# Four whole-expert weight buffers on SyncE's queue and the down weights on ScalarE's, in a mixture-of-experts layer

## The reference

```python
h = layer_norm(ALPHA * h + rglru_mixer(h), ...)
idx, w = route(h)                       # top 8 of 64 experts for each token
for block, e in blocks_of_rows_by_expert:          # routed experts
    gu = x[rows] @ w_gu[e]              # 1024 -> 2 x 256
    y = ((silu(gu[:, :256]) * gu[:, 256:]) @ w_down[e]) * row_weight
    acc = acc.at[rows].add(y)
ffn = acc + swiglu(x, sh_w_gu, sh_w_down)          # the shared expert
h = layer_norm(ALPHA * h + ffn, ...)
```

## Time and profile before

| | us |
|---|---|
| median of three runs | 1255.48 |
| the three runs | 1253.23 to 1258.09 |
| profiled execution, its own time | 1257.67 |
| its span | 1255.8 |
| mean granted TensorE clock, of full speed | 0.983 |
| TensorE matmul busy | 1190.0 |
| VectorE busy | 787.9 |
| GpSimd busy | 604.0 |
| ScalarE busy | 421.6 |
| gate/up weight loads (128 of 1 MB) | 8.4 median to landing |
| down weight loads (64 of 1 MB) | 9.0 median to landing |

### The profile page before, as it was taken

How to read it: one execution, slowest core, us unless ns; L and a number is a source line. 1 busy time by engine, 2 the same in 40 slices (tenths; PEclk the granted TensorE clock), 3 DMA queues, 4 the chain that set the end, 5 groups by cost and what they waited for, 6 DMA issues and landing times.

```text
span 1255.8 us, 22625 instructions
## 1 busy us (share of the span) xinstructions
PE 1190.0 (95%) x7122; PEld 1040.9 (83%) x7122; DVE 787.9 (63%) x1625; ACT 421.6 (34%) x582; POOL 604.0 (48%) x509
## 2 busy tenths in 40 slices
PE   6999999999999699999999999999999999999983
PEld 6897989747874289999999999999999998988941
DVE  7565647288987155666666666565666656647638
ACT  5253434353441023233233233232232232323323
POOL 5222222001657356556556656565666656646310
PEclk9999999999999999999999999999999999999987
DMA  6111111403341799999999999999999999999854
GB/s 240 51 35 51 49 35 34 188 22 135 104 166 40 277 321 335 380 363 358 376 360 353 374 355 353 357 355 360 348 355 353 343 353 347 345 341 315 273 132 177
DMA packets 83587, 317.50 MB, mean 253 GB/s; under 512 B 15989, under 2 KB 32450, under 8 KB 58594
## 3 DMA queue, kind: packets, MB, share of 16 engines
q1 hardware_dynamic: 56592, 249.50, 51.3%
q0 software_dynamic: 26656, 67.23, 21.9%
q10 hardware_dynamic: 306, 0.34, 0.1%
HBM read 274.38 MB, written 51.00 MB: 259 GB/s over the span
## 4 chain that ended last, share of the span: by engine, by line
DMA 49%; PE 24%; issue 11%; DVE 7%; POOL 3%; ACT 2%; POOLq 1%; DVEq 0%; ACTq 0%; SPq 0%
DMA routed_rows<-ysb,to_row 46%; PE bank L116 6%; PE bank L117 6%; PE bank L118 6%; PE bank L440 2%; PE bank L954 2%; POOL expert_list L784 1%; DMA xg<-h_rows,from_row 1%; PE bank L895 1%; POOL xg L809 1%; DMA win_raw<-in_w_in 1%; POOL routed_rows L839 1%; DVE routed L1437 1%; DVE routed L1426 1%; DVE h L1133 1%
## 5 line engine op out<-in xcount | busy, mean ns | idle before, releaser
L954 PEld LDWEIGHTS bank<-xT,wgu 128*128 128x128 f32 x4096 | 515.7, 191 | 24.3 <-issue 12.6
L954 PE MATMUL bank<-xT,wgu 128*128 128x160 f32 (+1 forms) x4096 | 520.2, 288 | 13.9 <-DVE sh L1230 11.8
L809 POOL DMA_INDIRECT xg<-h_rows,from_row x288 | 323.3, 1123 | 113.4 <-issue 86.4
L839 POOL DMA_INDIRECT routed_rows<-ysb,to_row x96 | 147.4, 1535 | 216.0 <-issue 211.3
L1095 ACT ACTIVATE ysb<-bank,of_row 128x512 f32<-128x512 f32 x64 | 44.0, 687 | 403.0 <-DVE to_row L1309 334.5
L1356 DVE TENSOR_TENSOR wd_lo<-wd_raw,wd_hi 128x1024 fp32r<-128x1024 f32 x128 | 151.2, 1222 | 35.9 <-ACT wd_hi L1086 35.4
L1086 ACT ACTIVATE wd_hi<-wd_raw 128x1024 fp32r<-128x1024 f32 x128 | 127.9, 1048 | 1.4 <-issue 0.6
L784 POOL DMA_INDIRECT expert_list<-entry,place x64 | 64.6, 1010 | 129.6 <-DVE place L1194 111.9
L116 PE MATMUL bank<-hT_hi,win_hi 128*128 128x348 f32 (+1 forms) x320 | 113.5, 355 | 9.6 <-DVE hT_lo L538 9.6
L116 PE MATMUL bank<-wd_hi,hid_hi 128*128 128x512 f32 x256 | 107.8, 421 | 7.3 <-DVE wd_lo L1356 7.2
L352 POOL TENSOR_TENSOR win_lo<-win_raw,win_hi 128x1024 fp32r<-128x1024 f32 x16 | 43.4, 2715 | 145.9 <-ACT win_hi L463 145.9
(11 more groups left out here) (216 smaller groups left out, 1640.3 us busy)
## 6 DMA issues: line engine op xcount, KB each, us to landing
wgu<-in_w_gu SPq DMA_DIRECT2D x128, 1024.0 KB, 8.4
wd_raw<-in_w_down SPq DMA_DIRECT2D x64, 1024.0 KB, 9.0
win_raw<-in_w_in SPq DMA_DIRECT2D x16, 512.0 KB, 3.9
xg<-h_rows,from_row POOLq DMA_INDIRECT x288
hT_raw<-in_hT SPq DMA_DIRECT2D x8, 520.0 KB, 7.8
wout_raw<-in_w_out SPq DMA_DIRECT2D x1, 4096.0 KB, 13.9
h_in<-in_h_rows SPq DMA_DIRECT2D x8, 512.0 KB, 4.0
h_rows<-h SPq DMA_DIRECT2D x8, 512.0 KB, 2.7
```

The costliest lines, as they stand in the source:

```text
L809: pool.indirect_dma_start(out=xg[b][:, g, :], out_offset=None, in_=h1_quarters, in_offset=bass.IndirectOffsetOnAxis(ap=from_row[b][:, g:g ...
L839: pool.indirect_dma_start(out=routed_rows, out_offset=bass.IndirectOffsetOnAxis(ap=to_row[b][0:r, half:half + 1], axis=0), in_=ysb[b][0:r, ...
L954: mm = pe.matmul(bank[:, 2 * f + half, 0:BLOCK[b]], wgu[b][:, f, k, c:c + P], xT[b][:, k, 0:BLOCK[b]], start=(k == 0), stop=(k == KT - 1))
```

## The change

Gate/up weights get four buffers of a whole expert. Two of them lie where `h1` and the mixer's tiles were, which is why SyncE waits for `h1_stored`, `routed_begun` and `turned` before it fills the third. One DMA of 2 MB loads an expert, on one semaphore, and that of block t+4 is asked for when up(t) is done. SyncE's step holds nothing else. The down weights of block t+2 are asked for by ScalarE, on its own DMA queue, as the last thing of its step t and after `down_done` of t; the first two are still SyncE's. At the start SyncE sends only the gate/up weights of block 0, waits for `lists_loaded`, then sends the down weights of 0 and the gate/up weights of 1 and 2; the gate/up weights of 3 go behind the rest of the lists. ScalarE's `gate(1)` goes ahead of its wait for `sched_stored`, VectorE's `gate_shared(1)` ahead of its first transpose. The loop's body is four steps instead of two, and the number of blocks is rounded up to a multiple of four; an empty block is added where that is needed (four more small VectorE instructions).

```diff
-T_MAX = 2 * (HALF + SEQ * TOP_K // P)
+BUFS = 4
+T_MAX = 2 * (HALF + SEQ * TOP_K // P) + 2
...
-    wgu = [m.at(f"wgu{j}", 16384 * j, [P, FT, KT, 2 * P], F32) for j in range(2)]
+    wgu_at = (0, 16384, 166432, 182816)
+    wgu = [m.at(f"wgu{j}", wgu_at[j], [P, FT, KT, 2 * P], F32) for j in range(BUFS)]
...
+    def wgu_loads(i, j):
+        return i * 16 // BUFS + j // BUFS * 16 + 16
...
+    def load_wd(eng, i, j):
+        e = of_block(eng, i + j, 1, E - 1)
+        eng.dma_start(wd_raw[j % 2][:, :, :],
+                      w_down[bass.ds(e, 1)].rearrange("o p k c -> p (o k) c")
+                      ).then_inc(wd_loaded[j % 2], 16)
...
-        n = eng.value_load(sched_i[0:1, 5:6], min_val=E - 4, max_val=T_MAX - 4)
-        with eng.Fori(0, n, 2) as i:
-            for b in range(2):
-                yield i, b, 4
-        for j in range(4):
-            yield n, j, 3 - j
+        n = eng.value_load(sched_i[0:1, 5:6], min_val=E - BUFS, max_val=T_MAX - BUFS)
+        with eng.Fori(0, n, BUFS) as i:
+            for j in range(BUFS):
+                yield i, j, 4
+        for j in range(BUFS):
+            yield n, j, BUFS - 1 - j
...
-        load_wgu(0, 0, 0)
-        load_wgu(0, 0, 1)
-        load_wd(0, 0)
-        load_wgu(0, 1, 0)
-        load_wgu(0, 1, 1)
+        load_wgu(0, 0)
+
+        sp.wait_ge(lists_loaded, 16 * NQ)
+        load_wd(sp, 0, 0)
+        load_wgu(0, 1)
+
+        sp.wait_ge(h1_stored, 16 * TILES)
+        sp.wait_ge(routed_begun, 16 * TILES)
+        sp.wait_ge(turned, TILES)
+        load_wgu(0, 2)
         sp.wait_ge(sh_up, 2 * FT)
-        load_wd(0, 1)
+        load_wd(sp, 0, 1)
...
+        load_wgu(0, 3)
...
-        for f in range(FT):
-            sp.wait_ge(up_done, UPS + 2 * f + 2)
-            load_wgu(0, 2, f)
         sp.wait_ge(sched_loaded, 16)
         for i, j, more in steps(sp):
-            for f in range(FT if more >= 3 else 0):
-                sp.wait_ge(up_done, (i + j) * UPS + 2 * UPS + 2 * f + 2)
+            if more >= 4:
+                sp.wait_ge(up_done, (i + j) * UPS + 2 * UPS)
                 sp.sem_inc(sp_pass, 1)
-                load_wgu(i, j + 3, f)
-            if more >= 2:
-                sp.wait_ge(down_done, DOWNS[1] + before(DOWNS, i, j + 1))
-                sp.sem_inc(sp_pass, 1)
-                load_wd(i, j + 2)
+                load_wgu(i, j + 4)
...
         act.dma_start(sched_dram[HALF:, :], sched_i[HALF:, 0:4]).then_inc(sched_stored, 16)
+        gate(1)
         act.wait_ge(sched_stored, 16)
...
-        gate(1)
...
+            if more >= 2:
+
+                act.wait_ge(down_done, DOWNS[1] + before(DOWNS, i, j + 1))
+                act.sem_inc(act_pass, 1)
+                load_wd(act, i, j + 2)
...
         rows_from(0, 1)
+        gate_shared(1)
         turn(0, 0)
         rows_from(0, 2)
-        gate_shared(1)
```

More of the change, by code:

```diff
@@ L73 @@
 HALF = E // 2
-T_MAX = 2 * (HALF + SEQ * TOP_K // P)
-assert T_MAX <= 2 * P
+BUFS = 4
+T_MAX = 2 * (HALF + SEQ * TOP_K // P) + 2
+assert T_MAX <= 2 * P and E % BUFS == 0
 UPS = 2 * FT
@@ L645, in stores_to @@
         return loads(i, j) * STORES[j % 2] + 16 * (j % 2)
+    def wgu_loads(i, j):
+        return i * 16 // BUFS + j // BUFS * 16 + 16
     def loads(i, j):
         return i * 8 + j // 2 * 16 + 16
-    wgu_loaded = [[sem(f"wgu_loaded{j}_{f}") for f in range(FT)] for j in range(2)]
+    wgu_loaded = [sem(f"wgu_loaded{j}") for j in range(BUFS)]
     wd_loaded = [sem(f"wd_loaded{j}") for j in range(2)]
@@ L679, in build @@
     sp_pass, pool_pass, pe_pass = sem("sp_pass"), sem("pool_pass"), sem("pe_pass")
-    dve_pass = sem("dve_pass")
+    dve_pass, act_pass = sem("dve_pass"), sem("act_pass")
+    def load_wd(eng, i, j):
[3 more added lines that the diff above has]
+                      ).then_inc(wd_loaded[j % 2], 16)
     def blocks_to_run(eng):
@@ L730, in experts_sp, with load_wgu @@
         sp.wait_ge(first_ready, 1)
-        def load_wgu(i, j, f):
+        def load_wgu(i, j):
             e = of_block(sp, i + j, 1, E - 1)
[L734 to L742, removed]
-        load_wgu(0, 0, 0)
-        load_wgu(0, 0, 1)
-        load_wd(0, 0)
-        load_wgu(0, 1, 0)
-        load_wgu(0, 1, 1)
+            sp.dma_start(wgu[j % BUFS][:, :, :, :].rearrange("p f k c -> p (f k c)"),
+                         w_gu[bass.ds(e, 1)].rearrange("o p f k c -> p (o f k c)")
+                         ).then_inc(wgu_loaded[j % BUFS], 16)
+        load_wgu(0, 0)
[6 more added lines that the diff above has]
+        load_wgu(0, 2)
         sp.wait_ge(sh_up, 2 * FT)
-        load_wd(0, 1)
+        load_wd(sp, 0, 1)
         sp.dma_start(sdn[:, :, :], sh_down.rearrange("(k p) c -> p k c", p=P)
                      ).then_inc(sdn_loaded, 16)
-        sp.wait_ge(listed, 16 * TILES * TOP_K)
         for q in range(NQ):
@@ L945, in up @@
             pe.sem_inc(pe_pass, 1)
+            pe.wait_ge(wgu_loaded[j % BUFS], wgu_loads(i, j))
+            pe.sem_inc(pe_pass, 1)
             for f in range(FT):
-                pe.wait_ge(wgu_loaded[b][f], loads(i, j))
-                pe.sem_inc(pe_pass, 1)
                 pe.wait_ge(hid_ready, (i + j) * FT + f + 1)
@@ L954, in up @@
                         mm = pe.matmul(bank[:, 2 * f + half, 0:BLOCK[b]],
-                                       wgu[b][:, f, k, c:c + P], xT[b][:, k, 0:BLOCK[b]],
+                                       wgu[j % BUFS][:, f, k, c:c + P], xT[b][:, k, 0:BLOCK[b]],
                                        start=(k == 0), stop=(k == KT - 1))
@@ L1262, in experts_dve @@
         gate_shared(0)
-        s.step(dve.tensor_scalar(sched_i[:, 4:5], ends[:, E - 1:E], 2.0, float(E), ALU.mult,
-                                 ALU.add))
-        s.step(dve.tensor_scalar(sched_i[:, 5:6], sched_i[:, 4:5], 4, None, ALU.subtract))
+        s.step(dve.tensor_scalar(sched_i[:, 4:5], ends[:, E - 1:E], 1.0, None, ALU.add))
+        s.step(dve.tensor_scalar(sched_i[:, 4:5], sched_i[:, 4:5], 1, 2, ALU.logical_shift_right,
+                                 ALU.logical_shift_left))
+        s.step(dve.tensor_scalar(sched_i[:, 5:6], sched_i[:, 4:5], E - BUFS, None, ALU.add))
+        s.step(dve.tensor_scalar(sched_i[:, 4:5], sched_i[:, 4:5], E, None, ALU.add))
         s.step(dve.tensor_scalar(done, ends, extra, None, ALU.is_le))
@@ L1278, in experts_dve @@
         s.step(dve.tensor_reduce(sc(3), part, AX, ALU.add))
-        s.step(dve.scalar_tensor_tensor(sc(2), sc(6), float(COLS), sc(3), ALU.mult, ALU.add))
+        s.step(dve.tensor_scalar(sc(7), sc(4), E - 0.5, float(E), ALU.is_gt, ALU.mult))
+        s.step(dve.tensor_tensor(sc(7), sc(7), sc(3), ALU.add))
+        s.step(dve.scalar_tensor_tensor(sc(2), sc(6), float(COLS), sc(7), ALU.mult, ALU.add))
         s.step(dve.memset(sc(0), float(E)))
```

## The result

The changed kernel takes 1277.22 us (median of 4 runs, 1272.97 to 1280.36) against 1255.18 us before on the same chip: a ratio of 1.0187, 95% interval 1.0165 to 1.0209. It is slower by 22 us in the medians, where 1249.5 was forecast. Its profiled execution took 1272.97 us, with a span of 1271.0 us (before: 1257.67 and 1255.8). That is the fastest of its four runs, while the profiled run of the kernel before lies above its median, so the two traces differ by 15.2 us only.

The account below looks back on a forecast made before the run. Bound by TensorE and the chain of stores, within a few per cent. Start -4.5, ScalarE +1, loop 0, tail -2.5 sum to -6 us: from 1255.48 to 1249.5 us, range 1239 to 1268.

Parts of the forecast that it names:

- What bounds the kernel: Steady loop: TensorE at 23.30 us a pair and the chain of stores, within a few per cent; 9.3 us lost.
- the loop's sum of 0 + 1 us: Steady loop: 0 us for buffers and larger loads, +1 us for ScalarE asking for the down weights.
- Part 1: Gate/up loads: four whole-expert buffers, one 2 MB load; removes a wait of zero, taken as 0 us.
- Part 2: Down weights asked for by ScalarE: each step 0.7 us later, mostly hidden; loads land in 7 to 8 us; +1 us.
- What hides it is VectorE's wait for the store: ScalarE's 0.7 us a step is covered by VectorE's 3.80 us wait before even `picks`; uncovered, 43 us.
- Rival A: Loop: stores pay for the second weight queue and 16 KB runs, 12 to 25 us on top, 1262 to 1275; chance 0.20.
- My objection in the rival: Against slower stores in the loop: total bytes are fixed, and turns weights take early they don't need later; no size.
- my row-by-row account of it in the rival: With both weight queues busy, a store's row waits 0.32 + 0.64 us instead of 0.32; nine rows give +5.8 us.
- Part 3: Start: fewer weights sent before the lists, so lists land sooner and block 2 begins earlier; -4.5 us, bounds -9 and +5.
- Rival C: Start gives nothing: gathers stand behind 5 MB, or the rest of the lists holds VectorE; 1254 to 1260; chance 0.14.
- Tail: Last pairs: the last gate/up load goes out earlier, so stores at 1150 to 1185 us run with less beside them; -2.5 us.
- Rival D: Four-step loop body fetches its code again: 15 rounds at some 2 us, +30 us, 1280; chance 0.04.

Follow-up runs that it names:

- e1: Changed kernel with the loop's down weights asked for by SyncE again, on its own queue: 1291.39 us, ratio 1.0301 to before.
- e11: Changed kernel with gate/up weights of block t+3 asked for after up(t+1), the old time; ScalarE's queue and 16 KB runs stay: 1279.72 us, ratio 1.0200.
- e10: Changed kernel with down weights back on SyncE's queue and whole gate/up loads (16 KB runs) asked for at the old times: 1255.83 us, ratio 1.0014.
- e5: Changed kernel with down weights back on SyncE's queue and gate/up loads split into 8 KB runs, early requests kept: 1273.18 us, ratio 1.0139.
- e8: Changed kernel with down weights back on SyncE's queue, 8 KB runs, and gate/up halves asked for at the old times: 1253.49 us, ratio 0.9994.
- e2: Changed kernel with each 2 MB gate/up load split into two of 1 MB with 8 KB runs: 1264.51 us, ratio 1.0084.
- e13: Changed kernel with gate/up weights asked for at the old times and ScalarE asking for down weights before its wait for ysb: 1276.10 us, ratio 1.0143.
- e3: Kernel before with only the loop's down weights asked for by ScalarE, on its own queue at the end of its step: 1284.81 us, ratio 1.0148.
- e4: Kernel before with only the change's new order of the start: 1254.13 us, ratio 1.0002.
- e7: Kernel before with all weight loads cut to 4 KB runs: 1263.22 us, ratio 1.0072.
- e6: Changed kernel with ScalarE asking for down weights before its wait for ysb: 1281.65 us, ratio 1.0221.

## Why the prediction was wrong, step by step

**What bounds the kernel: right, but without its time.** Two bounds within a few per cent, the chain of stores and TensorE, and the stores' time set by what loads beside them. What I missed is that the stores ran back to back in the first stretch too, and that a growing distance between them and TensorE, some 9 us in 30 blocks, hid it. Once that slack is used up, every delay of a store is a delay of the whole, and it is steep. One per cent on the round trips is 0.2 us a pair, nearly 7 us in 31 pairs.

**The step that failed: the loop's sum of 0 + 1 us.** It has the requests' new times and run length (part 1) at 0 and the second queue at nothing but ScalarE's own +1 (part 2). The loop from block 2 to block 62 took 21.0 us more. Either term was enough: with the second queue undone and the early requests kept the kernel is slower still (e1, 1.0301), with the early requests undone and the queue kept it is as slow (e11, 1.0200), and only with both undone is it level with before (e10, 1.0014).

**Part 1, the four buffers at 0.** I saw that a load asked for at t+4 removes no wait, and booked the earlier request at nothing. I looked only at when the weights are needed and not at what they collide with when they move. e5 against e8 prices it: 18 to 20 us with one queue. The run length I bounded by -9.3 us in all and +2.9 us a store and took as 0, because the engines' total share would stay as it is. The share did stay (0.99 to 1.02 in the first stretch of every kernel of the table); it is not what sets a store's time. 16 KB costs 0 to 2 us with the old request times (e8, e10), 18 with the early ones on one queue (e5, e1) and 13 with early ones on two (e2, after).

**Part 2, ScalarE: right in size for its own instructions, wrong in what it leaves out.** The waits of `wd_lo` for `wd_hi` rose from 31.8 to 65.0 us, 33 us over some 54 steps: 0.6 us a step for the forecast 0.7. "What hides it is VectorE's wait for the store" holds for most steps; TensorE still waits 15.1 us for `wd_lo` in 11 of them. I expected the loads to land in 7 to 8 us; it was 9.3, no faster than before: a queue of their own brought nothing while the engines' share stayed at 1.00. `wd_hi` waited for them twice at the start (5.8 us together) and not once between 500 and 1150 us, as forecast. The missing term is the queue itself: 16 to 23 us (e13 and e11 less e10 by their ratios), and e3 shows that it needs neither larger runs nor more buffers. A rival is that ScalarE's own time for the request is what costs, and no run issues on a second queue without ScalarE. The rows speak against it: in the changed kernel 44 of 56 stores between 480 and 1170 us start within 1.6 us of the landing before them, and 11 of the other 12 wait for GpSimd's gathers, so ScalarE's delay hardly reaches the chain of stores.

**Rival A named the cause and was given 0.20.** Its price, 12 to 25 us on top, was near: the result lies at 28, 4 of it the start given back. Its reason is only half right. The mean wait hardly grew: with two queues the sum of trips is 21.4 to 21.9 us in five kernels of six, hardly above 21.48 (22.3 in e3). It is the spread that grows: odd trips fall from 9.9 to 8.1 us and even ones rise from 11.6 to 13.3 us. A long trip holds everything up. A short one, in a machine that the stall has emptied, wins little, since GpSimd's own gathers then end later than the landing: the store behind an odd one starts more than 1.6 us after the landing in 11 of 28 cases (11 of 27 in e11, 1 of 29 before), and those odd trips average 6.3 us against 9.3 of the others. That adds 0.4 us a pair, which is the pair's whole rise from before to after (23.72 to 24.11). In e11, 1.14 us above before, the trips have 0.40 of it and the rest between them 0.74. Landing times of single DMAs between 480 and 1170 us lie between 7.6 and 11.1 us before, between 6.1 and 13.8 after, and between 6.0 and 14.3 in e13. My objection in the rival, that turns taken early aren't needed later, holds for the mean, and the mean alone doesn't set the pace. Why the second queue spreads the trips is not shown; my row-by-row account of it in the rival is not tested by any run.
The Trainium skill's page "DMA: Bandwidth & Descriptors", section "Issuing engines are not separate DMA queues", says that a second issuing engine saves only its issue time, as all DMAs interleave on the same 16 engines. The traces agree that it adds no bandwidth (344 GB/s in e11, 354 in e10), and show that it isn't neutral for a third party, the stores' queue: +1.9% here.

**Part 3, the start: right where it was measured, wrong in that it lasts.** Block 0 at 437.08 (437.5 forecast), block 2 at 461.11 (461). The list scatter landed in 4.87 us and the lists in 2.16. The 4.5 us were then summed as if the loop behind would pass them on. In the changed kernel block 0's store alone gave them back and 5.5 more; in e4, with nothing else changed, they are gone in the ratio, though its profiled execution ends with them. Rival C had this outcome, for other reasons.

**Tail**, -2.5: 1.2 us of it can be seen after y(63). **Rival D** is refuted: 21 instruction packets in q8 instead of 20, and e8 has the four-step body at 0.9994 of before.

**The whole.** The parts don't add: at the old request times the second queue costs about 20 us; at the early ones it gains 7 to 9 (e5 to e2) and 14 (e1 to after). Early requests cost 18 to 36 us with one queue and nothing with two. Why two queues damp this is open. The likely reading is that ScalarE's requests no longer go out together with SyncE's; no run tests it.

## What to carry to other kernels

Where a chain of small transfers paces a loop whose DMA engines are already full, every load beside it is a contender: its request time, its packet size and its queue can each cost, even where no wait for it is ever seen. Before asking for a load earlier or on another queue, look for a wait that it removes; a deeper buffer that nobody waits for was no gain here. Judge such a loop by the spread of the small transfer's round trip beside its mean, and find what comes last behind a short one (here GpSimd's gathers), since that keeps the gain. And compare the distance between the busiest engine and the chain at two places of the loop: where it grows, the chain is already the slower of the two.

## What the runs showed of the hardware

- The same bytes on two hardware queues instead of one: the share of the DMA engines' time is about the same (0.99 against 1.01), 344 against 354 GB/s, and single landing times of a store between 480 and 1170 us run from 6.0 to 14.7 us (e11) against 7.0 to 13.0 (e10).
- A contiguous run per partition is one packet up to 16 KB (3810 packets of 16 KB in the 62.42 MB of q1 after). The stores' median from 500 to 861 us is 9.0 us beside weight packets of 4 KB (e7) and 9.5 beside 8 KB (before). At the old request times with four buffers it is 9.7 beside 8 KB and 9.9 beside 16 KB (e8, e10), at the early ones on one queue 9.9 and 10.3 (e5, e1).
- From one store's issue through five gathers to the next store's issue GpSimd needed 8.7 us or more between 480 and 1170 us in every kernel of the table (8.72 at the least in the changed kernel and in e11).
- At the start, with two hardware queues, 16 KB runs and three gate/up loads outstanding, the second DMA of block 0's store took 21.0 us to land (20.3 in e6). With 8 KB runs, where the first of the three had landed by then, it took 11.1 (e2); with one queue, where one of the 2 MB loads is asked for 11 us later, 12.2 (e1). Each is one store. The next line is of the changed kernel between 455 and 480 us, the one after it of e1.

```profile
DMA to landing us min/median/max: 20.4/20.7/21.0
```

```profile
DMA to landing us min/median/max: 11.5/11.8/12.2
```
